# One barrier fewer between stages, direct stores of a layer's last rows, and a reordered setup in a two-layer decoder kernel

## The reference, cut to what matters

```python
for each of 2 layers:                                   # 512 tokens, model width 1024, float32
    p = rms_norm(x, g_mix) @ w_in                        # one input projection for three mixers
    x += concat(rwkv7(p), latent_attention(p), gated_mlp(p)) @ w_out
    x += memory_cross_attention(rms_norm(x), mem_k, mem_v)
    x += mixture_of_experts(rms_norm(x))                 # 32 experts, 2 chosen for each token
# once, before the layers:
kv    = rms_norm(mem, mem_norm_g) @ mem_w_kv             # 256 memory tokens
mem_k = rms_norm(kv[:, :256] by head, mem_k_g)
mem_v = kv[:, 256:]
```

## Time and profile before

| | |
|---|---|
| runs shown, median (lowest to highest) | 1950.03 us (1947.96 to 1954.32), 3 runs |
| the profiled execution: its own time | 1950.24 us |
| its span, from first to last instruction | 1948.5 us |
| setup block until the first matmul of layer 0 | 0 to 30.75 us |
| layer 0 until the first instruction of layer 1 | 30.7 to 954.2 us |
| layer 1 until the first instruction of the last block | 954.2 to 1923.9 us |
| the last block | 1923.9 to 1948.5 us |
| mean granted TensorE clock | 0.988 of full speed |

### The profile page before, as it was taken

The page is one execution under the profiler, slowest core; times in us unless marked ns, Lnnn a source line. Parts: engine busy times, 40 slices in busy tenths (PEclk is TensorE's granted clock), DMA queues, the critical chain, the costliest instruction groups (busy, mean ns, idle before and its releaser), DMA issues. The chain is left out here.

```text
span 1948.5 us, 24613 instructions
## 1 busy us (share of the span) xinstructions
PE 1827.8 (94%) x10238; PEld 928.3 (48%) x10238; DVE 650.9 (33%) x1235; ACT 402.0 (21%) x773; POOL 168.6 (9%) x212
## 2 busy tenths in 40 slices
PE   7989999999999999998799999999999999999986
PEld 4435875455444443333353469644554444334322
DVE  6357547135411111110233575541462111111102
ACT  3121345144000000000112324431540000000001
POOL 3000000002100000000300000010040000000001
PEclk9999999999999999999899999999999999999998
DMA  9502103321999999999740110051059999999996
GB/s 373 194 1 42 25 10 130 130 87 53 411 426 427 427 426 428 429 427 427 286 187 1 33 22 13 9 234 71 41 224 407 427 427 427 427 429 427 429 427 224
DMA packets 87810, 489.30 MB, mean 251 GB/s; under 512 B 45384, under 2 KB 50248, under 8 KB 60064
## 3 DMA queue, kind: packets, MB, share of 16 engines
q1 hardware_dynamic: 80288, 471.12, 59.0%
q0 software_dynamic: 7424, 16.78, 2.3%
HBM read 464.29 MB, written 31.98 MB: 255 GB/s over the span
## 5 line engine op out<-in xcount | busy, mean ns | idle before, releaser
L2024 PE MATMUL bank<-ring,hT 128*64 128x512 f32 x2080 | 474.4, 599 | 37.0 <-DMA ring<-in_we 31.2
L2024 PEld LDWEIGHTS bank<-ring,hT 128*64 128x64 f32 x2080 | 141.8, 137 | 319.1 <-issue 249.2
L1000 PE MATMUL bank<-hT,ring 128*128 128x512 f32 (+1 forms) x576 | 252.5, 599 | 0.0
L2031 PE MATMUL bank<-ring,arena 128*64 128x512 f32 x1040 | 236.7, 597 | 10.6 <-DMA ring<-in_we 8.5
L1000 PEld LDWEIGHTS bank<-hT,ring 128*128 128x128 f32 (+1 forms) x576 | 109.1, 191 | 139.8 <-issue 138.5
L2009 PE MATMUL bank<-shift_in,arena 128*128 128x256 bf16 (+2 forms) x1632 | 171.0, 262 | 0.0
L2009 PEld LDWEIGHTS bank<-shift_in,arena 128*128 128x128 bf16 x1632 | 140.6, 98 | 63.1 <-issue 48.9
L2070 DVE TENSOR_TENSOR hT<-bank,colp 128x512 f32<-128x512 f32 (+1 forms) x68 | 45.4, 668 | 351.9 <-PE bank L2009 339.2
L2387 ACT ACTIVATE arena<-bank 128x256 f32<-128x256 f32 x65 | 24.9, 382 | 603.4 <-PE bank L1995 603.4
L2031 PEld LDWEIGHTS bank<-ring,arena 128*64 128x64 f32 x1040 | 70.7, 137 | 143.3 <-issue 126.2
L2041 POOL DMA_INDIRECT expert_rows<-arena,row_places x64 | 62.6, 978 | 859.9 <-DVE arena L2523 845.4
(11 more groups left out here) (469 smaller groups left out, 1984.8 us busy)
## 6 DMA issues: line engine op xcount, KB each, us to landing
ring<-in_we SPq DMA_DIRECT2D x195, 2048.0 KB, 23.0
ring<-in_w_in SPq DMA_DIRECT2D x6, 2048.0 KB, 19.2
expert_rows<-ring SPq DMA_DIRECT2D x1, 8448.0 KB, 24.4
ring<-in_w_out SPq DMA_DIRECT2D x4, 2048.0 KB, 10.4
ring<-in_wm SPq DMA_DIRECT2D x2, 2048.0 KB, 8.5
ring<-in_w_in SPq DMA_DIRECT2D x2, 1920.0 KB, 16.5
ring<-in_w_in SPq DMA_DIRECT2D x2, 1664.0 KB, 27.1
ring<-in_w_in SPq DMA_DIRECT2D x2, 1152.0 KB, 28.9
```

The costliest lines, as they stand in the source:

```text
L1000: last = nc.tensor.matmul(B[n % 4][0:w, :], ins_units[unit][:, k, u0:u0 + w], hT[:, k, :], start=k == 0, stop=k == KD - 1)
L2024: last = nc.tensor.matmul(bank[CAP * j:CAP * j + CAP, :], x[:, k, :], up_w(u, j, k), start=k == 0, stop=k == KD - 1)
L2031: last = nc.tensor.matmul(bank[CAP * half:CAP * half + CAP, :], hid[u][:, m, :], down_w(slot, m, half), start=m == 0, stop=m == HM - 1)
```

## The change

There are three parts.

**Stages.** `leave_stage()` takes the place of `end_stage()` behind the setup block, the third block and the fourth block: no clear and no second barrier there, the stage's semaphores go on a list `late`. SP clears that list in the next block (`clear(late)`), and `release_late()` frees the names behind that block. The `end_stage()` behind the second block stays. Counters that were cleared for each layer now run on or have one semaphore for each layer. The body of the overflow branch now begins with a clear and a barrier of its own.

**Rows.** SP no longer waits for the stores at the end of the fourth block. POOL waits for them in the next block, ahead of the first gather (`rows_landed`). In layer 0 the rows of expert 31 are stored by two plain DMAs, one from SP and one from ACT (`store_last`), and not by the indirect one. `keep_busy` ahead of the combination is 3 matmuls, not 10.

**Setup.** PE runs 20 matmuls without a reader as soon as `ident` is there, then the first half of the keys, then the means of the memory, then the rest. ACT squares two tiles of x ahead of the roots, a third ahead of sine and cosine, the fourth behind. DVE sums the first tile ahead of the inversions, the second between the two scalings of keys.

```diff
+        def leave_stage():
+            late.extend(stage)
+            stage.clear()
+            late_held[0] = held[0]
+            held[0] = ExitStack()
+        def release_late():
+            late.clear()
+            late_held[0].close()
...
+        def rows_landed(eng, done):
+            eng.wait_ge(s_yo[0], 16 * (NE // 2) * done)
+            eng.wait_ge(s_yo[1], 16 * (NE // 2) * done - 16)
+            eng.wait_ge(s_yl, 32)
+            if done == DEPTH:
+                eng.wait_ge(s_yx, 32)
... DVE, setup
-                eng.wait_ge(s_mrt, 2)
-                v(eng.reciprocal(m_rs, m_rs))
-                eng.reciprocal(m_tok, m_tok).then_inc(s_mrr, 1)
...
+                sum_tokens(0)
+                eng.wait_ge(s_mrt, 2)
+                v(eng.reciprocal(m_rs, m_rs))
+                eng.reciprocal(m_tok, m_tok).then_inc(s_mrr, 1)
...
                 scale_keys(0)
-                sum_tokens(0)
+                sum_tokens(1)
                 scale_keys(1)
-                for i in range(1, NT):
+                for i in range(2, NT):
                     sum_tokens(i)
... ACT, setup
+                eng.wait_ge(s_ix, 16)
+                square_tokens(0)
+                square_tokens(1)
                 eng.wait_ge(s_mms, 1)
                 eng.activation(m_rs, B[0][:, 0:MEM], ACT.Sqrt, bias=epsc[:, 0:1]).then_inc(s_mrt, 1)
                 eng.activation(m_tok, B[1][:, 0:2], ACT.Sqrt, bias=epsc[:, 0:1]).then_inc(s_mrt, 1)
+                square_tokens(2)
                 eng.wait_ge(s_done, 1)
...
-                eng.wait_ge(s_ix, 16)
-                for i in range(NT):
-                    square_tokens(i)
+                square_tokens(3)
... PE, setup
                 eng.wait_ge(s_gc, 1)
+                for _ in range(20):
+                    nc.tensor.matmul(B[7][:, 0:P], ident[:, :], ident[:, :], start=True, stop=True)
+                eng.wait_ge(s_ik, 16)
+                keys(0)
                 eng.wait_ge(s_msm, 1)
...
                 last.then_inc(s_mms, 1)
-                eng.wait_ge(s_ik, 16)
-                keys(0)
                 keys(1)
...
-        end_stage()
+        leave_stage()
... the first block of a layer: SP, POOL, PE
                     if layer:
                         load_columns(eng, lay)
+                    clear(late)
+                    if layer:
                         eng.wait_ge(s_yg1[NT - 1], 16 * layer)
                         load_w_in(eng, lay, (1, 2, 0, 4, 5))
...
                     if layer:
+                        rows_landed(eng, layer)
                         combine_gather(eng, ys_d[0:NE * CAP, :])
...
-                        keep_busy(B[7], 10, 4 * P)
+                        keep_busy(B[7], 3, 4 * P)
... behind the third block: leave_stage() too; then the fourth block
+            def store_last(eng, half):
+                eng.wait_ge(s_ys, NE + 2)
+                eng.dma_start(ys_d[(NE - 1) * CAP:NE * CAP, 512 * half:512 * half + 512],
+                              ysb[1][CAP * half:CAP * half + CAP, :]).then_inc(s_yl, 16)
...
                         store_extra(eng)
-                        eng.wait_ge(s_yx, 32)
                     else:
...
-                    for z in range(2):
-                        eng.wait_ge(s_yo[z], 16 * (NE // 2) * (layer + 1))
+                        store_last(eng, 0)
...
-                    for e in range(NE):
+                    for e in range(NE if FINAL else NE - 1):
                         eng.wait_ge(s_ys, e + 3)
                         store_valid(eng, e % 2, e)
... ACT, at the end of its part of the fourth block
+                    else:
+                        store_last(eng, 1)
... behind the fourth block
-            clear(layer_sems)
-            end_stage()
+            leave_stage()
+            late.extend(layer_sems)
... the last block
             def _(eng):
+                rows_landed(eng, DEPTH)
                 combine_gather(eng, ys_d)
...
-                keep_busy(B[7], 10, 4 * P)
+                keep_busy(B[7], 3, 4 * P)
```

More of the change, by code:

```diff
@@ L122, in build @@
         s_yo = [ctx.enter_context(nc.semaphore(f"rows_written{u}")) for u in range(2)]
+        s_yl = ctx.enter_context(nc.semaphore("last_rows_written"))
+        s_yx = ctx.enter_context(nc.semaphore("extra_rows_written"))
+        s_rts, s_hs, s_rrs = [[ctx.enter_context(nc.semaphore(f"{x}_{z}")) for z in range(DEPTH)]
+                              for x in ("norm_root", "h_ready", "norm_factors")]
         layer_sems = []
@@ L528, in _, with square_tokens @@
                 eng.wait_ge(s_im, 16)
+                def square_tokens(i):
+                    if i >= 2:
+                        eng.wait_ge(s_xsm, i - 1)
+                    eng.activation(sqx[i % 2], xT[:, :, i * P:(i + 1) * P], ACT.Square).then_inc(s_xsq, 1)
                 for z in range(2):
@@ L587, in _ @@
                                      stop=True).then_inc(s_mk2, 1)
-        end_stage()
-        s_vc, s_ac, s_gp = layer_sem("dve_order_l"), layer_sem("act_order_l"), layer_sem("pool_order_l")
+        leave_stage()
+        s_vc, s_ac, s_gp = [ctx.enter_context(nc.semaphore(x)) for x in ("dve_order_l", "act_order_l", "pool_order_l")]
         vch, ach, gch = Chain(s_vc), Chain(s_ac), Chain(s_gp)
@@ L594, in build @@
             lay = slice(layer, layer + 1)
-            for chain in (vch, ach, gch):
-                chain.n = 0
+            s_rt, s_h, s_rr = s_rts[layer], s_hs[layer], s_rrs[layer]
+            pool_from = gch.n
             if layer:
@@ L675, in _ @@
                     eng.dma_start(brb[:, :], br_d[lay].broadcast_to([P, NG + NE])).then_inc(s_par, 16)
-                    eng.wait_ge(s_par, 16 * NPAR)
+                    eng.wait_ge(s_par, 16 * NPAR * (layer + 1))
                     if not layer:
@@ L1014, in _ @@
                             between[n]()
+            release_late()
             big = [ring[:, n, :].rearrange("p (h m t) -> p h m t", h=RH, m=4) for n in range(2)]
@@ L1786, in build @@
             SCX = float(RN) ** -0.5
+            memory_sems = list(stage)
             FINAL = layer == DEPTH - 1
@@ L1963, in build @@
             s_h2, s_h3 = sem("token_parts_2"), sem("token_parts_3")
-            s_yx = sem("extra_rows_written")
-            yo_done = 16 * (NE // 2) * layer
+            yo_done = [16 * (NE // 2) * layer, (16 * (NE // 2) - 16) * layer]
             def bc(ap, n):
@@ L2586, in _ @@
                         turn(GROUPS, 0, 0, False, False)
-            o_sem = {x: sem("more_" + x) for x in ("w", "sel", "g", "xr", "tx", "xg", "up", "hr", "th", "sg", "hid",
-                                                   "dn", "ys", "sp", "spt", "spc", "add")}
+            release_late()
+            o_sem = dict(zip(("w", "sel", "g", "xr", "tx", "xg", "up", "hr", "th", "sg", "hid", "dn", "ys", "sp", "spt",
+                              "spc", "add"), memory_sems))
             n_more = nc.values_load(more_n, min_val=0, max_val=MORE - 1)
             with nc.If(n_more > (1 if FINAL else 0)):
+                clear(o_sem.values())
+                nc.all_engine_barrier()
                 with nc.Fori(1 if FINAL else 0, n_more) as j:
@@ L2660, in _ @@
                             eng.wait_ge(o_sem["dn"], 1)
+                            eng.wait_ge(s_yo[0], 16 * (NE // 2) * (layer + 1))
+                            if FINAL:
+                                eng.wait_ge(s_yx, 32)
                             eng.tensor_copy(ysb[0], B[5][:, :]).then_inc(o_sem["ys"], 1)
```

13 lines of the change are left out of this document (4 added, 9 removed).

## The result

The changed kernel takes 1935.54 us (median of 4 runs, 1934.64 to 1936.84) against 1950.32 us; the ratio is 0.992 (95% interval 0.9905 to 0.9934). It is faster by 0.8%, more than the 0.3% that a measurement can tell and more than the 8.8 us of the forecast.

A forecast was written before the change was run, and what follows sets the result against it. PE, busy in 94% of the span, was taken to bound the kernel. Gains of 2.4 (setup), 1.1 (second barriers), 3.1 (turn) and 2.2 (end of layer 1) summed to 8.8 us: 1950.24 to 1941.4 us, range 1937.5 to 1947.5.

The forecast's parts named there:

- Setup: Before layer 0's first matmul: new order ends on DVE at 27.9, PE starts at 28.25, not 30.75; gain 2.4 us.
- Second barrier: Hand-over from third to fourth block, once per layer: dropping clears and second barrier saves 0.55 us each, 1.1 us.
- Turn: Layer 0 to layer 1: plain stores' flight lies beside a hand-over shortened to 2.75 us; gain 3.1 us.
- End of layer 1: After layer 1's last stores: landing lies beside a shortened hand-over, gather at 1922.5, not 1924.74; gain 2.2 us.
- Shorter `keep_busy`: Matmuls at the turn, ahead of the transposes: their length is worth nothing, the clock 1.7 us either way; value 0.
- rival D: Turn to layer 1: the clock rises earlier, 1.7 us more gained, 1939.7 us; chance 0.10.
- B: Block hand-overs: not hidden or shortened, 3.3 and 2.2 us from the last issue; gain 6.4, 1943.8 us; chance 0.17.
- C: Setup: x-bound and longer, leaving 0.5 of the 2.4 us; total gain 6.9, 1943.3 us; chance 0.10.
- F: Head of layer 1: gaps after three matmuls keep PE at 1.2 GHz, slower, 1956 us; chance 0.04.

The follow-up runs named there:

- before_three: Kernel before with 3 matmuls ahead of the combination instead of 10, nothing else: 1948.45 us (0.9987).
- ten_matmuls: Changed kernel with 10 matmuls ahead of the combination instead of 3: 1938.26 us (0.9946).
- filled kernels: Changed kernel and kernel before, each with matmuls without a reader in two projection-block gaps where PE waits for ACT: 1932.6 us (0.9914) and 1945.12 us (0.9977).
- indirect_last: Changed kernel with expert 31's rows in layer 0 stored by POOL's indirect DMA again, without the plain stores there: 1938.39 us (0.9941).

## Why the prediction was wrong

Step by step, in its own terms (the first pair of profiles, then what the runs add):

- Setup, 2.4: measured 3.2, and 3.5 against the mean of the old setups. Mechanism and order right, PE's end 26.8 (forecast 26.9) and DVE's 27.27 (forecast 27.9), since x landed a little earlier (16.19, not 16.35) and operations followed each other more closely than their lengths, added up, say. The size was off, and the kernel before happened to have its shortest setup in the profile shown.
- Second barrier, 2 x 0.55: the hand-overs got 0.41 and 0.37 us shorter, 0.8 and not 1.1. The columns mix 0 and mix 1 have 0.3 and 0.7, with what the third block of layer 1 gave.
- Turn, 3.1: measured 3.5. The sum was near, the mechanism mis-weighted. The forecast put the 3.3 us between landing and block down to the barriers, the walk through the overflow count and the clears, and kept 2.75 of them. 1.4 of them were POOL's DRAIN behind its indirect store, and the clears with the second barrier were worth 0.8 here. The hand-over from the last issue on took 1.8 (944.44 to 946.25), and then the landing ended last. The price of the plain store was looked for in its landing time only. That is indeed no shorter (2.4 and 2.6 against 2.3), so the first-byte difference that the Trainium skill states ("DMA: Bandwidth & Descriptors", Latency and other measured facts) does not show here either.
- End of layer 1, 2.2: measured 2.0. Right; the landing ends last there too.
- Shorter `keep_busy`, 0 within 1.7: measured 1.3 at the head. This is the smaller failure: rival D's mechanism, with 0.10, is what happened. The shorter count may have part in it (1 us in before_three, one profile), the shorter idle time ahead of it the rest; ten_matmuls keeps the short head with ten matmuls.
- What failed most is a step that was not in the sum: "So the change is worth only what it takes out of places where PE has nothing to do, or where something else ends a stage", that is, stages whose code stays were taken to keep their time. The last 3.4 us (1.6 in proj 1, 1.8 in mix 1) are dips of the clock behind gaps of 1.2 to 3.4 us. The granted clock was read at the head of layer 1 only. A look at the whole span of the kernel before would have shown five more dips in layer 1, each with up to 1.7 us to win or lose, and a range widened by two of them on each side would have held the time.

Against the forecast's 8.8 us the first pair of profiles has 14.4. Of the 5.6 between them, 3.4 are these dips, 1.3 the head, 0.8 the setup and 0.4 the turn, less 0.3 at the hand-overs and at the end. Without the dips the time would have been about 1939, inside the range.

Rivals B and C did not occur: the hand-over from the last issue on took 1.8 and 1.5 us, not 3.3 and 2.2, and the setup was not x-bound beyond the forecast. F did not occur either: the low stretch ended with PE's dense work (granted 0.50 from 960 to 965 us, 0.98 from 965 to 970). That activity releases the array's throttle is what the Trainium skill states ("TensorE: Matmul & The Clock Gate", Part 1: The HAM clock gate), and rows 12 and the stretches above agree.

Structure and chance add up: 3.5 setup, 1.0 in mix 0 and mix 1, 3.5 turn, 1.5 head and 2.0 end are 11.5, beside the 12.5 us between the filled kernels' medians. The 14.8 between the first medians contains chance; over all sets of unaltered runs the medians differ by 12 to 16.

What remains open is why proj 1 had two dips in both profiles of the kernel before and one in both of the changed kernel. The dips follow no instruction that the change touched. But none of the eight profiles of the changed kernel and its variants with the gaps open has two there (seven have one, indirect_last none), and before_three, whose layer starts otherwise, has one. The means of all unaltered runs (1950.3 of 58, 1936.3 of 8) lie 13.9 us apart, 1.6 more than those of the filled kernels (12.3). So the 1.6 of proj 1 may come with the new start of layer 1 and not by luck. No run tests this. For mix 1 it was luck.

## What to carry to other kernels

Read the granted clock over the whole span before giving a sum: a gap of 1 to 3 us in front of dense matmuls can cost 1.7 us more than itself in one execution and nothing in the next, and a matmul without a reader in the gap takes this chance away (3 to 4 us here). Where a block ends, end it on plain DMAs from SP or ACT and let the consumer wait for the landing: POOL's DRAIN held the block until 1.3 to 1.4 us behind the landing of its last indirect store, whether another engine waited for it or not. When two chains share engines ahead of a stage, start with the one whose data lands first, and see which engine ends last after it.

## What was not expected of the hardware

- A block whose last work is POOL's indirect DMA is left 3.6 us behind its issue, with plain DMAs 1.8 us. POOL's DRAIN outlasts the landing by 1.3 to 1.4 us. Even in the changed kernel it is what opens the turn's barrier, by the store of expert 30 that was issued 6 us earlier.
- The turn of before_three took 10.4 us against 7.7 in three other profiles of the old turn. PE's sequencer spent 3.37 us in the jump over the overflow branch (0.44 in the kernel before), with an instruction load of 0.02 MB beside it that the first profile does not have at that place, and the second barrier waited for PE. One case; why the load fell there is open.
- The kernel before had five dips of the clock behind the head of layer 1 in one execution and three in the next. A kernel without a change gave 1943.32 to 1956.52 us over its runs.
